# Last block of w_down in three token passes, its output stored from two queues, and the second norm's squares summed on VectorE

## What is computed

```
h     = rmsnorm(x, g_mix);   proj = h @ w_in              # 2048 -> 3072: u | v | z
out_a = gelu(u) * (tril(W_s) @ rmsnorm_head(gelu(v)) + b) # chunks of 128 tokens
out_b = (trailing means of z over 2/4/8/16 tokens - z) @ w_pool * pool_scale
x     = x + concat(out_a, out_b) @ w_out                  # x1
h     = rmsnorm(x, g_ffn)                                 # "the second norm"
x     = x + square(relu(h @ w_up)) @ w_down               # 2048 -> 8192 -> 2048
out   = rmsnorm(x, g_final)
```

## Time and profile before

| | us |
|---|---|
| runs, unprofiled | 1257.12, 1275.77, 1485.61 (median 1275.77) |
| profiled execution, its own time | 1256.82 |
| its span, slowest core (core 3) | 1255.3 |
| spans of the eight cores | 1252.3 to 1255.3, granted PE clock 0.989 to 0.991 |
| busy share: PE, DVE, ACT, POOL | 96%, 27%, 20%, 5% |

### The profile page before, as it was taken

The page is one execution under the profiler, slowest core; times in us unless marked ns, Lnnn a source line. Parts: engine busy times, 40 slices in busy tenths (PEclk is TensorE's granted clock), DMA queues, the critical chain, the costliest instruction groups (busy, mean ns, idle before and its releaser), DMA issues.

```text
span 1255.3 us, 14349 instructions; the slowest of 8 cores (1252.3 to 1255.3 us)
## 1 busy us (share of the span) xinstructions
PE 1206.0 (96%) x5736; PEld 547.6 (44%) x5736; DVE 335.0 (27%) x550; ACT 252.0 (20%) x473; POOL 66.3 (5%) x97
## 2 busy tenths in 40 slices
PE   5899999899999999999999999999999999999994
PEld 2354444344444444444444444444444444444441
DVE  3565556312112121211112121212121121211234
ACT  2401287223321110001111000111100011123332
POOL 0100000000000000000000000000000000000000
PEclk9999999899999999999999999999999999999997
DMA  8995510987656445545554554455455545559985
GB/s 272 228 176 83 83 37 2 158 165 147 133 79 83 74 67 85 82 68 73 83 80 67 79 85 72 68 84 85 68 72 86 78 68 77 87 83 141 144 170 172
DMA packets 37921, 126.95 MB, mean 101 GB/s; under 512 B 2784, under 2 KB 2912, under 8 KB 36832
## 3 DMA queue, kind: packets, MB, share of 16 engines
q0 software_dynamic: 24912, 95.43, 51.9%
q1 hardware_dynamic: 12944, 30.61, 7.9%
HBM read 213.05 MB, written 8.39 MB: 176 GB/s over the span
## 4 chain that ended last, share of the span: by engine, by line
PE 92%; ACT 2%; DMA 2%; DVE 2%; issue 1%; SPq 1%; DVEq 0%; ACTq 0%
PE ps L217 81%; PE ps L652 8%; DMA xf<-xT 2%; PE ps L404 1%; PE ps L842 1%; SPq L235 0%; ACT L589 0%; PE ps L316 0%; ACT sqv L599 0%; DVE xr_h L808 0%; DVE xr_mid L808 0%; PE ps L682 0%; PE ps L681 0%; PE ps L355 0%; ACT pooled L569 0%
## 5 line engine op out<-in xcount | busy, mean ns | idle before, releaser
L217 PE MATMUL ps<-h2T,ringall 128*128 128x512 bf16 x2048 | 442.8, 379 | 0.0
L217 PEld LDWEIGHTS ps<-h2T,ringall 128*128 128x128 bf16 x2048 | 200.4, 98 | 241.6
L217 PE MATMUL ps<-pooled,ringall 128*128 128x512 bf16 x1024 | 234.1, 379 | 0.0
L217 PE MATMUL ps<-uT,ringall 128*128 128x512 bf16 x1024 | 234.1, 379 | 0.0
L767 DVE SCALAR_TENSOR_TENSOR rtmp<-ps,rstd_bc 128x512 f32<-128x512 f32 x128 | 82.5, 686 | 360.9 <-PE ps L217 351.2
L217 PEld LDWEIGHTS ps<-pooled,ringall 128*128 128x128 bf16 x1024 | 100.2, 98 | 120.8
L217 PEld LDWEIGHTS ps<-uT,ringall 128*128 128x128 bf16 x1024 | 100.2, 98 | 120.8 <-issue 0.3
L772 ACT ACTIVATE uT<-rtmp 128x512 bf16<-128x512 f32 x64 | 39.1, 629 | 505.9 <-DVE rtmp L767 505.9
L217 PE MATMUL ps<-hT,ringall 128*128 128x512 bf16 x384 | 83.7, 379 | 0.0
L772 ACT ACTIVATE pooled<-rtmp 128x512 bf16<-128x512 f32 x64 | 39.3, 629 | 181.7 <-DVE rtmp L767 181.7
L652 PE MATMUL ps<-uT,ringall 128*128 128x512 bf16 x256 | 60.1, 390 | 4.4 <-DVE uT L545 4.4
(11 more groups left out here) (98 smaller groups left out, 527.8 us busy)
## 6 DMA issues: line engine op xcount, KB each, us to landing
ringall<-w_down POOLq DMA_DIRECT2D x40, 1024.0 KB, 10.5
ringall<-w_up POOLq DMA_DIRECT2D x32, 1024.0 KB, 10.5
ringall<-w_in POOLq DMA_DIRECT2D x10, 1024.0 KB, 12.0
xf<-xT SPq DMA_DIRECT2D x8, 1024.0 KB, 20.9
ringall<-w_out POOLq DMA_DIRECT2D x8, 1024.0 KB, 15.8
xstage<-xT SPq DMA_DIRECT2D x16, 512.0 KB, 13.3
wstg<-w_in SPq DMA_DIRECT2D x4, 1024.0 KB, 16.1
outT<-xr_h SPq DMA_DIRECT2D x16, 256.0 KB, 4.0
```

The source lines that it names most:

```text
L217: ins = e.matmul(ps[:, banks[sel], c0:c1], lhsT, rhs, start=st, stop=sp_)
```

## The change

Five things.

1. **Second norm.** Tile 0's squares are written in float32 to `sqacc`; those of tiles 1 to 13 to one float32 buffer `sqf`, and `accumulate` adds them to `sqacc` on DVE (13 additions of 128x1024), each queued on DVE behind the next tile's L659. ACT's square of tile m waits for the addition of tile m-1, since `sqf` is single. After the 13th addition DVE makes two bf16 tiles of the sum, high part and rest, and PE multiplies both by ones (4 matmuls). Tiles 14 and 15 go to PE as before (4 matmuls). The first relu of the MLP also waits for the last addition, since `rtmp` shares memory with `sqf`.
2. **Loads of the closing block.** Its 8 slabs are loaded once. Five go to the ring; the last six column tiles (three 1 MB loads) go to `wres`, which lies where h2T was, and wait for the last up job.
3. **Passes.** The closing block runs over tokens 0 to 511, 512 to 767 and 768 to 1023. The matmuls of the second and third pass are 256 tokens wide.
4. **Scaling.** In the first two passes one DVE instruction (scalar_tensor_tensor) multiplies by g_final and rstd; ACT's multiplication stays in the last pass alone.
5. **The end.** rstd of the last pass is written to PSUM for DVE and again to SBUF for POOL. DVE scales 12 tiles in 5 instructions (256, 256, 512, 1024, 1024 elements for each partition) and POOL 4 tiles in two of 512 elements, into a new buffer `ostage`. SP stores three groups and ACT four. The output tensor is [128, 16*1024], each pass's block with its rows of one partition next to each other; the host puts it in order.

```diff
+PASSES = ((0, 512), (512, 768), (768, 1024))
+NRES = 6
-        for j in range(8):
+        for j in range(8 if fb < NFB - 1 else NSLOT):
             slabs.append(w_down_d[:, 16 * fb + 2 * j:16 * fb + 2 * j + 2, :, :])
-    for j in range(8):
-        slabs.append(w_down_d[:, 16 * (NFB - 1) + 2 * j:16 * (NFB - 1) + 2 * j + 2, :, :])
...
+        if sq_wait:
+            accumulate(sq_wait.pop())
+        first, direct = m == 0, m >= SQ_DIRECT
+        dst = sqacc if first else sq_end[m - SQ_DIRECT] if direct else sqf
+        sq = P.add("act", lambda e: e.activation(out=dst[:, :], in_=XR(m)[:, :], func=AF.Square), [x1_e[1][m], acc_last[0]])
...
+    def accumulate(item):
+        m, sq = item
+        acc_last[0] = P.add("dve", lambda e: e.tensor_tensor(out=sqacc[:, :], in0=sqacc[:, :], in1=sqf[:, :], op=ALU.add), [sq, acc_last[0]])
+        if m == SQ_DIRECT - 1:
+            hi = P.add("dve", lambda e: e.tensor_copy(out=sqr[:, 0, :], in_=sqacc[:, :]), [acc_last[0]] + hs_reader)
+            lo = P.add("dve", lambda e: e.tensor_tensor(out=sqr[:, 1, :], in0=sqacc[:, :], in1=sqr[:, 0, :], op=ALU.subtract), [hi])
...
+    issue_loads(NSLAB - 1)
+    up_last = slab_done[nlast - 1]
+    for j in range(NRES // 2):
+        wres_ld.append(P.dma("pool", lambda e, j=j, t0=t0: e.dma_start(out=wres[:, 2 * j:2 * j + 2, :, :], in_=w_down_d[:, t0:t0 + 2, :, :]),
+                             "wres%d" % j, [up_last]))
...
+    def final_out(i, k):
+        o = P.add("dve", lambda e: e.scalar_tensor_tensor(out=XR(k)[:, t0:t1], in0=XR(k)[:, t0:t1], scalar=vecs[:, G_FIN + k:G_FIN + k + 1],
+                                                          in1=rstd_bc[:, t0:t1], op0=ALU.mult, op1=ALU.mult), [rexp[i], x3_ops[i][k], cst])
+        P.dma("sp", lambda e: e.dma_start(out=out_block(i, k, 1), in_=XR(k)[:, t0:t1]), "st", [o])
...
+    for i, (t0, t1) in enumerate(PASSES):
+        for m in range(KC):
+            segs = [([(0, 0, T, down_w(m, k), MIX(k)[:, t0:t1], k == 0, k == FB - 1) for k in range(FB)], [down_ld(m), act_ops[FB - 1]])]
...
+        if lastp:
+            exp_ps = P.add("act", lambda e, t0=t0, t1=t1: e.activation(out=rps, in_=rstd_bc[:, t0:t1], func=AF.Exp, scale=-0.5), [ln, bank_last[7]])
+        rexp[i] = P.add("act", lambda e, t0=t0, t1=t1: e.activation(out=rstd_bc[:, t0:t1], in_=rstd_bc[:, t0:t1], func=AF.Exp, scale=-0.5), [ln])
...
+    for eng, m0, n in (("dve", 0, 1), ("dve", 1, 1), ("pool", lo0, 2), ("dve", 2, 2), ("dve", 4, 4), ("pool", lo0 + 2, 2), ("dve", 8, 4)):
+        tail_ops[m0] = (n, P.add(eng, lambda e, m0=m0, n=n, rs=rs: e.tensor_tensor(
+            out=ostage[:, m0:m0 + n, :], in0=xr_group(m0, n), in1=rs.unsqueeze(1).broadcast_to([128, n, T]), op=ALU.mult),
+    for queue, sem, starts in (("sp", "st", (0, 2, 8)), ("act", "sta", (1, lo0, 4, lo0 + 2))):
```

More of the change, by code:

```diff
@@ new lines, in stat_sum, with fn, mk @@
+    def stat_sum(parts, start, stop, deps):
+        def fn(e):
+            ins = None
+            for i, p in enumerate(parts):
+                for half in range(2):
+                    ins = e.matmul(ps[:, 6 + half, :], ones[:, :], p[:, half * 512:(half + 1) * 512], start=start and i == 0, stop=stop)
+            return ins
+        return P.add("pe", fn, deps)
+    def accumulate(item):
[4 more added lines that the diff above has]
+            lo = P.add("dve", lambda e: e.tensor_tensor(out=sqr[:, 1, :], in0=sqacc[:, :], in1=sqr[:, 0, :], op=ALU.subtract), [hi])
+            def mk():
+                pe = stat_sum([sqr[:, 0, :], sqr[:, 1, :]], True, False, [hi, lo, ones_op, bank_last[6], bank_last[7]])
+                hs_reader[:] = [pe] * 4
+                return pe, m
+            pend.append(mk)
@@ L800, in build_program @@
         prev_down_last = dj
[L802 to L813, removed]
+    nlast = nbase + (NFB - 1) * 16 + 8
@@ L832, in build_program @@
             bank_last[banks[0]] = ev
+            x3_ops[i][m] = ev
             hsl = hs_ctr[0] % 4
             hs_ctr[0] += 1
[L835 to L838 removed]
+            sq_ap = sqr[:, hsl // 2, (hsl % 2) * 512:(hsl % 2) * 512 + T]
@@ L839, in mk @@
+            sq = P.add("act", lambda e, m=m, sq_ap=sq_ap, t0=t0, t1=t1: e.activation(out=sq_ap, in_=XR(m)[:, t0:t1], func=AF.Square), [ev, hs_reader[hsl]])
+            def mk(m=m, sq=sq, sq_ap=sq_ap, hsl=hsl, T=T, sbank=sbank):
                 d = [sq, ones_op]
                 if m == 0:
-                    d.append(bank_last[6 + half])
-                pe = P.add("pe", lambda e: e.matmul(ps[:, 6 + half, :], ones[:, :], sq_ap, start=(m == 0), stop=(m == KC - 1)), d)
+                    d.append(bank_last[sbank])
+                pe = P.add("pe", lambda e: e.matmul(ps[:, sbank, 0:T], ones[:, :], sq_ap, start=(m == 0), stop=(m == KC - 1)), d)
@@ L845, in build_program @@
             pending[0] = mk
[L846 to L849, removed]
+            if lastp:
+                pre_ops[m] = P.add("act", lambda e, m=m, t0=t0, t1=t1: e.activation(out=XR(m)[:, t0:t1], in_=XR(m)[:, t0:t1], func=AF.Copy,
+                                                                                    scale=vecs[:, G_FIN + m:G_FIN + m + 1]), [ev, sq, cst])
@@ L854, in build_program @@
-        rexp[half] = P.add("act", lambda e, c0=c0, c1=c1: e.activation(out=rstd_bc[:, c0:c1], in_=rstd_bc[:, c0:c1], func=AF.Exp, scale=-0.5), [ln])
-    for k in range(KC):
-        final_half_out(k, 1)
+        bank_last[sbank] = ln
+        if lastp:
+            rps = ps[:, 7, 0:T]
+            exp_ps = P.add("act", lambda e, t0=t0, t1=t1: e.activation(out=rps, in_=rstd_bc[:, t0:t1], func=AF.Exp, scale=-0.5), [ln, bank_last[7]])
+        rexp[i] = P.add("act", lambda e, t0=t0, t1=t1: e.activation(out=rstd_bc[:, t0:t1], in_=rstd_bc[:, t0:t1], func=AF.Exp, scale=-0.5), [ln])
@@ L858, in build_program @@
+    for queue, sem, starts in (("sp", "st", (0, 2, 8)), ("act", "sta", (1, lo0, 4, lo0 + 2))):
+        for m0 in starts:
+            n, o = tail_ops[m0]
+            P.dma(queue, lambda e, m0=m0, n=n: e.dma_start(out=out_block(len(PASSES) - 1, m0, n), in_=ostage[:, m0:m0 + n, :]), sem, [o])
     keys = P.finalize()
@@ L941 @@
         b, q = divmod(c, 4)
-        out[b, q * TOK:(q + 1) * TOK, :] = np.asarray(res.results[c]["outT"], np.float32).T
+        o = np.asarray(res.results[c]["outT"], np.float32)
+        for t0, t1 in PASSES:
+            blk = o[:, KC * t0:KC * t1].reshape(128, KC, t1 - t0)
+            out[b, q * TOK + t0:q * TOK + t1, :] = blk.transpose(2, 1, 0).reshape(t1 - t0, D)
     return out
```

82 lines of the change are left out of this document (52 added, 30 removed).

## The result

| | before | changed kernel |
|---|---|---|
| runs compared, us | 1257.12, 1256.48 | 1245.37, 1246.94, 1248.45 |
| profiled execution: spans of the eight cores | 1252.3 to 1255.3 | 1240.4 to 1243.8 |
| ratio, with its 95% interval | | 0.9921, 0.9892 to 0.9951 |

The changed kernel is 0.8% faster, 10 us, and the interval does not reach 1. The prediction had 1246 us. In some executions two or more cores show a mean granted clock of about 0.97 or less and the run is some 27 us longer or more, whatever the kernel; the comparisons leave these runs out, and spans of "undisturbed cores" are those of cores at a clock of 0.987 or more, from all runs. Over the whole study these give 1253.0 us for before (282 spans, standard deviation 1.3) and 1242.9 us for the changed kernel (28, 1.6).

The account below looks back on a forecast made before the run. PE was taken to bound the kernel, its tail a serial chain of small instructions, then stores. Against the profiled 1256.8 us, -5.2 + 0.5 + 0.7 + 1.3 - 7.8 = -10.5 gave 1246 us, range 1241 to 1265.

Parts of the forecast that it names:

- 24 sums taken from PE, less the wait: w_out loop: 24 fewer sums on PE save 5.2 us, 0.5 us lost waiting; net -4.7, between -5.2 and -1.
- loads once: Closing block: dropping eight 1 MB loads is worth 0, since PE never waited for one there.
- pace at 256 columns: Closing block, passes 1 and 2: 109.2 ns for each 256-column matmul, +0.7 us in all.
- new seam: Closing block, between passes 1 and 2: PE waits for addition, square and sums; +1.3 us, bounds 1.0 and 1.8.
- tail after PE's last job: End of the kernel: 11.6 us after PE's last job in place of 19.4, a gain of 7.8 us.
- the high end of the range: Whole time: 1265 us, from 1246 + 19, since before's median run stands 19 us above its profiled one.
- bare weight loads: Rival, closing block: 256-column matmuls don't hide their loads, 205 ns each, 52 us more, 1298 us; chance 0.04.
- The wait for x: w_out loop's end: a late x load delays the first up job or the sum of the rest; 0.5 us, bounds 0 and 4.2.
- PE comes there about 3.9 us earlier and 2 us are left: w_out loop, tile 11's banks: without 9 sums PE's 6 us in hand shrinks to 2, no stall.
- The loop paced by x: Rival, w_out loop: x loads keep the 15.1 us cycle, so the first part gains nothing, 1251 us; chance 0.12.
- The tail that stays: Rival, end: stores of the short last pass held by POOL or latency, tail 16 us, 1251 us; chance 0.10.
- POOL hidden: End: POOL's two 512-element scalings, estimated 1.1 us each, set the end only if over 5 us together; cost nothing.

Follow-up runs that it names:

- e1: Changed kernel with the second norm back on PE, squares in bf16, two sums per tile; ratio to before 0.9951, undisturbed cores 1247.3 us against 1242.9.
- e3: Kernel before with one edit, the closing block's 8 slabs loaded once; ratio to before 0.9994, undisturbed cores 1252.4 us against 1253.0.
- e4: Changed kernel with its last pass scaled by 16 DVE instructions and stored by 16 transfers from SP; undisturbed cores 1245.0 us, tail 12.29 us against 9.57.
- e5: Changed kernel with the last seven stores all issued by SP; tail after the last sum 9.48 us against 9.57.
- e7: Changed kernel with each pass's last sum emitted behind the next pass's first job; undisturbed cores 1239.2 us against 1242.9, one undisturbed run 1241.5 us.
- e6: Changed kernel with POOL's two scalings given to DVE; tail after the last sum 9.70 us against 9.57; core 4 took 1247.5 us, other undisturbed cores 1240.5 to 1243.0.
- e9: Changed kernel with passes of 512, 384 and 128 tokens; undisturbed cores 1240.5 us against 1242.9, tail 6.33 us.

## Why the prediction was right or wrong

**The sum held.** Each term of it, against the stages above:

| term | predicted | measured |
|---|---|---|
| 24 sums taken from PE, less the wait | -5.2 + 0.5 | -4.9 (and 5.1 to undo it, e1) |
| loads once | 0 | 0 to -0.6 (e3) |
| pace at 256 columns | 109.2 ns | 109 ns |
| new seam | +1.3 | +1.2 |
| closing block to its last sum, from these and the narrower chain ahead of the sum (-0.5) | +1.5 | +1.6 |
| from PE's last job to the first scaling | 2.8 us | 2.6 us |
| tail after PE's last job | 11.6 us | 10.8 us |
| time | 1246 | 1245.4 to 1248.5, median 1246.9 |

**The step that failed is what the forecast was held against.** The sum of the costs was right; the kernel before that it was set beside was not. The prediction closed its sum with the sentence that the median of the runs, 1275.8, "lies 19 us higher, and nothing in the profile explains that", and built on it twice: the high end of the range (1265), and 0.07 for faster by over 2%, "1246 is 2.3% under 1275.8". Whoever reads 1246 against 1275.8 expects a gain of 30 us, 2.3%; the gain is 10, 0.8%. The runs showed in its place a kernel before of 1256 us: the twenty executions of it that the comparisons use lie between 1255.3 and 1257.1, and of its other runs none but this one lies under 1282. Its clocks are not listed, so what held it up is open. The profiled execution's own 1256.8 was the only basis, and against it the sum's forecast was -0.8%. A high end of 1254, where the bounds of the costs ended, would have held the time. (The lower of the bounds is 1243.6 when added up, and not 1243; nothing hangs on it.)

**Two per cent was too coarse.** The text took 2% for what a measurement can tell and put 0.88 within it. The interval came out at 0.3% to either side, so the gain of 0.8% is distinct from none. The chances by 2% say nothing false, but they hide that the sum said faster with little doubt: of the rivals, only bare weight loads (0.04) made the kernel slower.

**Terms that were mis-sized.**

*The wait for x, 0.5 us.* It is 0 on nearly every core: e1 stands 5.2 to 5.3 us above e4, e5 and e7 in the first stage, and no core of the changed kernel's profiled execution waits. It is not 0 everywhere: on core 4 of e6 it cost 5 us, over the bound of 4.2. It came where the prediction looked for it, at the sum of the rest, for which it had 1 us; the wait was 3.55 us, and the prediction had no term for the clock after a wait. The step "PE comes there about 3.9 us earlier and 2 us are left", on the banks, was wrong. It let PE run ahead of x by all the nine sums before that place, but the loads are issued by the same loop and come earlier with it; what goes is the time of three jobs' sums, 3 x 0.43 = 1.3 us. On core 3 of before DVE took a product 7.9 us after it was ready and the bank was free 6.5 us before PE came for it; on core 4 of the changed kernel, the one with the latest loads (up to 12.6 us), these are 8.0 and 5.1 us.

*The tail, 0.8 us too long.* The chain to the first scaling was 0.2 shorter; the rest is the rate. The 2.10 MB moved in some 5.8 us, 360 GB/s (an estimate, with the first slices; 361 to 430 in the full ones of core 6), for the 315 taken from the earlier trace rows. That 315 was one core's. e3 has the stores and the layout of before, and its core 1 kept 340 to 393 GB/s in the full slices (of 0.5 us, from 1232 us), while its core 5 fell to 205:

```profile
GB/s 365 45 0 0 0 0 12 369 143 0 0 0 16 295 377 393 393 356 385 385 389 389 361 389 381 389 385 360 377 385 381 340 348 352 348 217 12 0 0 0
```

So neither the new layout nor the groups are needed for such a rate. What makes one core slower than another is open.

**The rivals.** The loop paced by x is excluded by e1, as the rule of the loop; single late loads remain (e6). The tail that stays is excluded by the profile after: 10.8 us. Bare weight loads are excluded at 256 columns (109 ns) and, by e9, at 128 (59 ns); the Trainium skill's sentence on row groups (TensorE: Matmul & The Clock Gate, Part 3, The mechanism) does not hold for this stream, where load and matmul use all rows and still overlap.

**Right for a reason that was not the one given.** The prediction had POOL hidden because it ends before DVE. It does: two scalings of 512 in 2.49 us, 1.25 each. The estimate from the Trainium skill (GPSIMD Engine Reference, 3.1 Elementwise) was 1.1 us; the measured value decides. But e6 shows that even DVE's end can come 1.2 us later and change nothing. Neither engine sets the end, the bytes do, as long as the issues keep ahead of them (e4).

## What to carry to other kernels

Cut the span at instructions that both kernels have and compare stage by stage: a change of 0.8% is then four differences, each many times its scatter, while the total drifts by 1 us from stages that nobody touched. What is left after the last matmul is bounded by the bytes of the last pass, so make that pass narrow, until its tiles are shorter than the chain through the other engines; and group the stores so that their issue stays ahead of the transfers. A seam at which PE waits for a sum can be filled for nearly nothing: emit the sum behind the next job (2.6 of 3.0 us came back). And before work is moved from the busy engine to an idle one, look at what it will stand behind there: the sum on DVE stands behind an addition that waits for a load, and now and then that wait reaches PE. Read such slack from every core, not from one.

## What the runs showed that I had not expected

- Landing times belong to the core and the moment. Over the whole kernel the same 512 KB loads of x had medians from 9.0 (core 5) to 13.3 us (core 3) within one execution of before, and from 8.4 to 11.6 in the changed kernel. A comparison of core 3 before with core 6 after (13.3 and 11.2) would have shown a gain that isn't there.
- A second store queue and a second scaling engine changed the tail by 0.1 and 0.1 us, within the scatter, while seven stores in place of sixteen changed it by 2.7.
- In the changed kernel's profiled execution core 6 had a granted clock of 0.94 in one stretch of 10 us inside a full stream, where core 3 had 1.00; from 246.9 on 16 matmuls came 260 to 264 ns apart in place of 216, 0.8 us in all with those at its edges, and the granted clock of 247 to 251 was 0.81. Core 7 has the same 0.81 there. The stretch, in the columns of the earlier trace rows:

```profile
240.00:250.00 10.00, 9.95 (x44) 4.42 (x44) 0.08 (x1) 2.09 (x2) 0.55 (x1) 0.94 1.01 175
```

PE was busy throughout (9.95 of 10 us), so no wait goes with this fall, unlike the one in e6. What causes it is open.
